# A feed-forward of 11 chunks with three pairs of chunks in Strassen's scheme instead of two

## The reference

```python
def swiglu(h, w_gate, w_up, w_down):          # w_gate, w_up: 1024 x 2816, w_down: 2816 x 1024
    return (jax.nn.silu(h @ w_gate) * (h @ w_up)) @ w_down

for l in range(DEPTH):                        # DEPTH = 2
    x = x + 0.5 * swiglu(rms_norm(x, ffn1_norm[l]), ffn1_w_gate[l], ffn1_w_up[l], ffn1_w_down[l])
    h = rms_norm(x, mix_norm[l])
    z = h @ w_in[l]                           # -> q, k, v of 8 heads, and p
    ...
    x = x + jnp.concatenate([a, m], axis=-1) @ w_out[l]
    x = x + 0.5 * swiglu(rms_norm(x, ffn2_norm[l]), ffn2_w_gate[l], ffn2_w_up[l], ffn2_w_down[l])
return rms_norm(x, final_norm)
```

## Time and profile before

| | |
|---|---|
| median of 3 runs | 915.77 us |
| profiled execution | 916.29 us, of which the span of the trace 914.50 us |
| granted clock of TensorE | 0.999 of full speed |
| busy share of the span | PE 99%, PEld 81%, DVE 77%, ACT 59%, POOL 5% |
| DMA | 180.76 MB, mean 198 GB/s |

### The profile page before, as it was taken

One profiled execution on the slowest core, in us unless ns is written; L12 is line 12 of the kernel. 1 busy time (PEld: TensorE's weight loads), 2 busy tenths in 40 slices (PEclk: granted clock), 3 DMA queues, 4 the chain that ended last, 5 costly groups with the idle time before them and its releaser, 6 DMA issues.

```text
span 914.5 us, 12693 instructions
## 1 busy us (share of the span) xinstructions
PE 905.3 (99%) x4217; PEld 741.0 (81%) x4217; DVE 704.0 (77%) x946; ACT 539.3 (59%) x793; POOL 47.1 (5%) x78
## 2 busy tenths in 40 slices
PE   8999999999999999999999999999999999999997
PEld 6788888887878888888888888888877888888886
DVE  5999599459757998597489986975787588968954
ACT  6775366457638566465385655644675496555633
POOL 1010010010001010100010101010100001001000
PEclk9999999999999999999999999999999999999999
DMA  7966747755245857675267676676434277675831
GB/s 244 347 170 233 275 92 278 240 176 186 93 126 166 307 116 277 213 216 211 92 227 280 141 278 199 207 235 232 138 141 145 84 265 230 218 273 118 274 116 47
DMA packets 131101, 180.76 MB, mean 198 GB/s; under 512 B 7664, under 2 KB 107296, under 8 KB 131056
## 3 DMA queue, kind: packets, MB, share of 16 engines
q1 hardware_dynamic: 117744, 165.43, 52.4%
q0 software_dynamic: 9984, 11.22, 7.4%
q10 hardware_dynamic: 3328, 3.54, 1.2%
HBM read 179.11 MB, written 2.07 MB: 198 GB/s over the span
## 4 chain that ended last, share of the span: by engine, by line
PE 94%; DMA 2%; DVE 2%; ACT 1%; SPq 1%; issue 1%; POOLq 0%; DVEq 0%; POOL 0%; ACTq 0%
PE ps L1397 28%; PE ps L1400 28%; PE ps L1398 28%; PE ps L1506 2%; DMA w_raw<-in_ffn_w_up_dram 1%; PE ps L1458 1%; PE ps L1407 1%; PE ps L1408 1%; PE ps L1480 1%; PE ps L1696 1%; PE ps L1712 1%; PE ps L1724 1%; PE ps L1740 1%; DMA w_raw_f<-in_ffn_w_up_dram 1%; SPq L376 0%
## 5 line engine op out<-in xcount | busy, mean ns | idle before, releaser
L984 DVE TENSOR_TENSOR w_lo<-w_raw,w_hi 128x1024 fp32r<-128x1024 f32 x184 | 216.5, 1218 | 86.4 <-ACT w_hi L627 85.9
L627 ACT ACTIVATE w_hi<-w_raw 128x1024 fp32r<-128x1024 f32 x168 | 167.2, 1049 | 91.0 <-PE ps L1400 91.0
L1397 PE MATMUL ps<-w_hi,gt_hi 128*128 128x512 f32 (+1 forms) x356 | 138.8, 390 | 0.0
L1398 PE MATMUL ps<-w_lo,gt_hi 128*128 128x512 f32 (+1 forms) x356 | 137.7, 387 | 0.0
L1397 PE MATMUL ps<-w_hi,xs_hi 128*128 128x512 f32 x288 | 114.0, 396 | 0.0
L1400 PE MATMUL ps<-w_hi,xs_lo 128*128 128x512 f32 x288 | 112.4, 390 | 0.0
L1398 PE MATMUL ps<-w_lo,xs_hi 128*128 128x512 f32 x288 | 112.2, 390 | 0.0
L1397 PE MATMUL ps<-w_hi,xt_hi 128*128 128x512 f32 x272 | 110.0, 404 | 1.0 <-DVE xt_lo L1009 0.8
L1400 PE MATMUL ps<-w_hi,gt_lo 128*128 128x512 f32 (+1 forms) x356 | 109.8, 387 | 0.0
L1398 PE MATMUL ps<-w_lo,xt_hi 128*128 128x512 f32 x272 | 106.1, 390 | 0.0
L1400 PE MATMUL ps<-w_hi,xt_lo 128*128 128x512 f32 x272 | 101.0, 391 | 0.0
(11 more groups left out here) (151 smaller groups left out, 1487.9 us busy)
## 6 DMA issues: line engine op xcount, KB each, us to landing
w_raw<-in_ffn_w_down_dram SPq DMA_DIRECT2D x72, 512.0 KB, 5.4
w_raw<-in_ffn_w_gate_dram SPq DMA_DIRECT2D x62, 512.0 KB, 4.6
w_raw<-in_ffn_w_up_dram SPq DMA_DIRECT2D x62, 512.0 KB, 5.7
w_raw<-in_w_in_dram SPq DMA_DIRECT2D x32, 512.0 KB, 4.7
w_raw_f<-in_ffn_w_gate_dram SPq DMA_DIRECT2D x16, 512.0 KB, 5.3
w_raw_f<-in_ffn_w_up_dram SPq DMA_DIRECT2D x16, 512.0 KB, 6.2
w_raw_e<-in_ffn_w_down_dram SPq DMA_DIRECT2D x16, 512.0 KB, 7.0
w_raw<-in_w_out_dram SPq DMA_DIRECT2D x16, 512.0 KB, 5.2
```

The source lines that it names most:

```text
L627: nc.scalar.activation(w_hi[slot][:, part], w_raw[raw][:, part], ACT.Copy).then_inc(hi_ready[slot], 2)
L984: nc.vector.tensor_tensor(w_lo[slot][:, part], w_raw[raw][:, part], w_hi[slot][:, part].bitcast(F32), ALU.subtract).then_inc(lo_ready[slot ...
L1397: nc.tensor.matmul(o, hi, wh, start=start, stop=False)
L1398: nc.tensor.matmul(o, hi, wl, start=False, stop=False)
```

## The change

The 11 chunks are dealt in another way: ordinary are 0, 1, 2, 5 and 8, and the pairs are 3+4, 6+7 and 9+10. Each pair now has one ordinary chunk ahead of it, whose transposes and down product lie inside the pair, and the last pair ends the feed-forward. The pair's seven products, seven combines and their order are the same. The loop is gone on all engines: the rounds are written one after the other. Which unit lies in which raw tile and which split place is read from two tables, `RAWS` and `SPLITS`; in the loop the places repeated with each body.

At the end, the down product of chunk 8 does only its first token tile between T2 and T3; its second comes after T4, in two parts with the transposes of `gated_x` between them and those of `gated` behind. The split of `d9` is cut in its two halves on DVE. Smaller: places e and f swap their addresses; the final norm's gain is loaded into a raw tile that has become free, when the last pair's third sum is done; the load of the pooling matrix moves to the start of each mix stage, that of the mask into `load_params`; the loads of the attention bias wait for the last pair's T3.

```diff
-SLOT_E, SLOT_F = 3, 4
-BODIES = 2
-N_ORDINARY = 3 + 2 * BODIES
+SLOT_F, SLOT_E = 3, 4
+PAIRS = 3
+N_ORDINARY = 2 + PAIRS
...
+SPLITS = dict(a=("0a", "1a", "B21.0", "T4.0", "B21.1", "T4.1", "B21.2", "T4.2", "d10"),
...
+              e=("2a", "B11.0", "T2.0", "5a", "B11.1", "T2.1", "8a", "B11.2", "T2.2", "d9"),
...
+RAWS = dict(a=("0a", "1a", "B11.0", "d3", "B22.1", "8a", "B12.2"),
...
+SUM_IN = dict(T1="B11", T2="B11", T3="B12", T4="B21")
+SPLIT_OF = {unit: (role, k) for role in SPLITS for k, unit in enumerate(SPLITS[role])}
+RAW_OF = {unit: (role, k) for role in RAWS for k, unit in enumerate(RAWS[role])}
...
-        final_gain = sb("final_gain", [P, D_MODEL])
+        sb("feed_forward_rest", [P, D_MODEL])
+        final_gain = w_raw[FF2["d"]][:, 0:D_MODEL]
...
+                summed(0, 2)
+                gate_up("5a", 5, 0)
+                split("d2")
+                gate_up("5b", 5, 1)
+                summed(0, 3)
+                down(3)
+                split("T3.0")
+                down(4)
+                split("T4.0")
+                gate_up("B11.1", 7, 0)
...
+                          (gu_ready[1], ord_no(layer, ff, j + 3) + 1))
+                unit(f"d{following}", (down_used, down_no(layer, ff, y + 2)))
+            def last_pair(layer, ff):
+                j, x, y = PAIRS - 1, LAST - 1, LAST
+                n = pair_no(layer, ff, j)
+                pair_begun(layer, ff, j)
+                split_unit(layer, ff, f"d{x}", (m_ready, 7 * n + 5))
+                act.wait_ge(combined, 7 * n + 4)
+                silu_pair(p1, 0, 1)
+                if (layer, ff) == (DEPTH - 1, FF2):
+                    load_final_gain(layer, ff)
+                act.wait_ge(combined, 7 * n + 6)
+                silu_pair(m5, 1, 0)
+                act.wait_ge(combined, 7 * n + 7)
+                silu_pair(u, 1, 1)
+                store_gt_hi(layer, ff, x, 1)
+                split_unit(layer, ff, f"d{y}", (m_ready, 7 * n + 7))
+                store_gt_hi(layer, ff, y)
...
+            def add_units(layer, ff, into, other):
+                tile = w_raw[raw_of(layer, ff, into)[0]]
+                nc.vector.tensor_tensor(tile[:, :], tile[:, :],
+                                        w_raw[raw_of(layer, ff, other)[0]][:, :], ALU.add
+                                        ).then_inc(sum_ready, 1)
...
+            def first_sum(layer, ff, j):
+                slot, n = raw_of(layer, ff, f"B12.{j}")
+                dve.wait_ge(raw_ready[slot], raw_count(slot, n))
+                split_done(layer, ff, f"B11.{j}")
+                add_units(layer, ff, f"B11.{j}", f"B12.{j}")
...
+                o = 3 * j + 2
                 dve.wait_ge(sum_ready, 3 * n + 1)
-                dve.wait_ge(lo_ready[f], 4 * unit_no(layer, ff["stage"], f, 3 * j) + 5)
-                add_units(e, b)
-                lo(d, 3 * j + 2, d)
-                lo(e, 3 * j + 1, e)
-                store_gt_lo(layer, ff, i)
+                split_done(layer, ff, f"T1.{j}")
+                add_units(layer, ff, f"B11.{j}", f"B22.{j}")
+                unit(layer, ff, f"d{o}")
+                unit(layer, ff, f"T2.{j}")
+                store_gt_lo(layer, ff, o)
+                dve.wait_ge(sum_ready, 3 * n + 2)
+                split_done(layer, ff, f"B21.{j}")
+                add_units(layer, ff, f"B21.{j}", f"B11.{j}")
                 dve.wait_ge(m_copied, 2 * n + 1)
                 dve.wait_ge(m_ready, 7 * n + 3)
                 combine(c11, ps[:, BANK_X, :], p1, ALU.add)
...
                 combine(m5, m5, u, ALU.subtract)
                 dve.wait_ge(combined, 7 * n + 3)
                 combine(p1, ps[:, BANK_Z, :], m5, ALU.add)
-                lo(a, 3 * j + 4, a)
+                unit(layer, ff, f"T4.{j}")
                 gate_pair(p1, gated_x, 0, 1, 4 * n + 2)
-                lo(e, 3 * j + 2, b)
+            def second_column(n):
...
+            def ff_body(layer, ff, j):
+                x, y, following = 3 * j + 3, 3 * j + 4, 3 * j + 5
+                n = pair_no(layer, ff, j)
+                pair_begun(layer, ff, j)
+                unit(layer, ff, f"{following}a")
+                second_column(n)
+                unit(layer, ff, f"{following}b")
+                gate_pair(m5, gated_x, 1, 0, 4 * n + 3)
+                last_block(n)
+                unit(layer, ff, f"d{x}")
                 gate_pair(u, gated, 1, 1, 4 * n + 4)
-                store_gt_lo(layer, ff, i + 1, 1)
-                lo(d, 3 * j + 3, e)
-                store_gt_lo(layer, ff, i + 2)
-                gate(layer, ff, 2 * j + 3, 0)
-                lo(a, 3 * j + 5, a)
-                gate(layer, ff, 2 * j + 3, 1)
-                lo(b, 3 * j + 5, b)
+                store_gt_lo(layer, ff, x, 1)
+                unit(layer, ff, f"d{y}")
+                unit(layer, ff, f"B21.{j + 1}")
+                store_gt_lo(layer, ff, y)
+                unit(layer, ff, f"B11.{j + 1}")
+                gate(layer, ff, j + 3, 0)
+                first_sum(layer, ff, j + 1)
+                gate(layer, ff, j + 3, 1)
+                unit(layer, ff, f"B22.{j + 1}")
+                unit(layer, ff, f"T1.{j + 1}")
+            def last_pair(layer, ff):
+                x, y = LAST - 1, LAST
+                n = pair_no(layer, ff, PAIRS - 1)
+                pair_begun(layer, ff, PAIRS - 1)
+                slot, m = split_of(layer, ff, f"d{x}")
+                raw = raw_of(layer, ff, f"d{x}")[0]
+                split_lo(slot, m, raw=raw, halves=(0,))
+                second_column(n)
+                gate_pair(m5, gated_x, 1, 0, 4 * n + 3)
+                last_block(n)
+                split_lo(slot, m, raw=raw, halves=(1,))
+                gate_pair(u, gated, 1, 1, 4 * n + 4)
+                store_gt_lo(layer, ff, x, 1)
+                unit(layer, ff, f"d{y}")
+                store_gt_lo(layer, ff, y)
...
+            def transpose_x(layer, ff, j):
+                pe.wait_ge(pair_gated, 4 * pair_no(layer, ff, j) + 3)
+                transpose_tiles(gated_x)
+            def transpose_y(layer, ff, j):
+                pe.wait_ge(pair_gated, 4 * pair_no(layer, ff, j) + 4)
+                pe.wait_ge(gt_lo_ready, gt_no(layer, ff, 3 * j + 3) + 1)
+                transpose_tiles(gated)
+            def pair(layer, ff, j):
                 n = pair_no(layer, ff, j)
-                units = (3 * j + 2, 3 * j + 2)
-                ordinary(layer, ff, 2 * j + 2, 0, (a, b), units)
-                transpose_gated(layer, ff, 2 * j + 1)
-                ordinary(layer, ff, 2 * j + 2, 1, (a, b), units)
-                whole_down(layer, ff, i - 1, d, 3 * j + 1)
+                o = 3 * j + 2
                 pe.wait_ge(x_lo_ready, 4 * ff_no(layer, ff) + 4)
...
+                seventh(layer, ff, BANK_X, f"B11.{j}", A11)
...
+                seventh(layer, ff, BANK_X, f"B21.{j}", A12)
...
+                seventh(layer, ff, BANK_Y, f"T2.{j}", S2)
+                whole_down(layer, ff, o, ts=(0, 1) if j < PAIRS - 1 else (0,))
                 pe.wait_ge(combined, 7 * n + 2)
-                seventh(layer, ff, BANK_Y, f, 3 * j + 1, S3)
+                seventh(layer, ff, BANK_Y, f"T3.{j}", S3)
                 pe.wait_ge(combined, 7 * n + 1)
-                seventh(layer, ff, BANK_X, a, 3 * j + 4, A22)
-                units = (3 * j + 2, 3 * j + 2)
...
+                seventh(layer, ff, BANK_X, f"T4.{j}", A22)
...
+                ordinary(layer, ff, 2, 0, 2, {4: lambda: transpose_gated(layer, ff, 1)})
+                ordinary(layer, ff, 2, 1, 2)
+                whole_down(layer, ff, 1)
+                pair(layer, ff, 0)
+                for j in range(1, PAIRS):
+                    x, y, o = 3 * j, 3 * j + 1, 3 * j + 2
+                    n = pair_no(layer, ff, j - 1)
+                    pe.wait_ge(combined, 7 * n + 4)
+                    ordinary(layer, ff, j + 2, 0, o)
+                    transpose_x(layer, ff, j - 1)
+                    pe.wait_ge(combined, 7 * n + 6)
+                    ordinary(layer, ff, j + 2, 1, o, {4: lambda: transpose_y(layer, ff, j - 1)})
+                    whole_down(layer, ff, x, buf=1)
+                    whole_down(layer, ff, y)
+                    pair(layer, ff, j)
+                x, y = LAST - 1, LAST
+                whole_down(layer, ff, LAST - 2, ts=(1,),
+                           after={(1, 0): lambda: transpose_x(layer, ff, PAIRS - 1)})
+                transpose_y(layer, ff, PAIRS - 1)
+                x_slot, n = split_of(layer, ff, f"d{x}")
```

456 lines of the change are left out of this document (217 added, 239 removed).

## The result

The changed kernel takes 909.32 us (median of 4 runs, 908.38 to 910.0); the kernel before, run beside it, took 915.88. The ratio is 0.9927, 95% interval 0.9915 to 0.9939: 6.6 us faster, where 909.3 was predicted.

> The changed kernel itself, for a ratio on the same chip as the two kernels beside it: 909.3 within 0.7 us.

What follows compares the result with a forecast made beforehand. The prediction took PE (TensorE) as the bound: 914.50 - 10.9 (matmuls) - 0.3 (refills) + 4.5 (end waits) = 907.8 us span, 909.6 with 1.79 around it, less 0.3: 909.3 us. Range 904.2 to 915.

Steps and rivals of the forecast that it cites:

- What goes: In each feed-forward 12 fewer matmuls at 0.227 us, 10.9 us in all, and one refill less, 0.3 us.
- What covers the added Vector work: In the rounds Vector's 42.4 us plus up to 5 us of waits fit PE's 47.6 us; priced at 0.
- the first transition: From pair 3+4 to chunk 5, the tightest place: Vector comes 0.7 us ahead of PE at 5b; priced at 0.
- Vector's busy time: Over the kernel, Vector's busy time rises from 704 to about 761 us.
- The wait at the end: Before the transposes of gated, PE waits 1.13 us per feed-forward for Vector's chain, 4.5 us in all; bounds 0 and 8.5.
- Loop to straight code: At the loop's jumps, leaving the loop is worth 0 on PE, as the trace shows no gap there.
- Loads: Raw units and the mix stage's first weights land in time, priced at 0; late loads would cost 23 us.
- The sum: Over the whole span, 914.50 - 10.9 - 0.3 + 4.5 = 907.8 us, giving a predicted time of 909.3 us.
- No wait at the ends: At each feed-forward's end Vector is ahead and the 4.5 us wait is absent: 904.8 us; chance 0.17.
- Small waits in the rounds: At the first transition Vector lacks 0.7 to 2 us, so PE waits in 4 places: 912 to 917 us; chance 0.16.
- Vector sets the rounds: In the 12 rounds Vector's work and waits exceed PE's 47.6 us by 1.5 us: 927 us; chance 0.12.
- The change doesn't deliver: Across many places PE waits as much as the removed matmuls save: 914 to 916 us; chance 0.05.

Runs made afterwards that it cites:

- the second experiment: The kernel before with its loop of two bodies written out on SP, ACT, DVE and PE, nothing else: 915.74 us, ratio 0.9997.
- the first experiment's second run: Rerun of the changed kernel with d9's two half splits moved later on Vector, behind the combines and the gt_lo: 906.21 us, ratio 0.9892 (first run 906.1 us).
- the last version: Changed kernel with d9's half splits later on Vector, T2 rounded before Scalar's second copy, gated_x transposed before d8's second tile: 903.62 us, ratio 0.9867.
- that kernel: The changed kernel with d8's down product whole between T2 and T3, and the transposes of gated_x and gated right behind T4: 917.95 us, ratio 1.0020.

## Why the prediction was right, and where it was not

*What goes.* 48 matmuls at 0.227 us: shown by count (528 in a line) and by worth, since the experiment with fewer matmuls gained in the middle pair their pitch, 2.0 to 2.1 us for nine (no wait appears there).

*What covers the added Vector work.* Shown in the changed kernel (no wait of PE in any round) and by its limit: 2.27 us more at one place of each round come out almost whole in the first round of a feed-forward and not at all in the others. The tightest place is 5b at the first transition, as the prediction had it, but with less to spare. In the second feed-forward:

```profile
348.31 2.35 DVE L1080 TENSOR_TENSOR w_lo_f<-w_raw,w_hi_f 128x1024 fp32r<-128x1024 f32 x2
349.79 0.40 PE L1516 MATMUL ps<-w_hi_f,xs_hi 128*128 128x512 f32 x1
```

A half of a split is 1.22 long, so the first half is done at 349.53, 0.26 us ahead of the matmul; 0.7 was forecast. Read in the same way, the leads there are 0.5 at T2 and 1.0 at T4 and at 5a, for 0.9, 1.4 and 1.4: the order of the places is right, and each lead is 0.4 smaller. Half of that lies where the chain starts (B11's split begins 1.44 us behind the release of its place, 1.25 was reckoned); the rest was not traced. The next two feed-forwards have the same leads, and in the first the one at 5b is 0.05. So the price of 0 came out right with very little to spare. T1, where the extra work shows first, has 0.7 to 0.9 and is not in the prediction's list. (Of the four splits that the section on the change counts behind a pair's first `gt_lo`, its rows show three, `d4`, B21 and B11; `d3` stands ahead of it.)

*Vector's busy time.* Its size was wrong: I counted one sum of units more for each feed-forward, but a pair needs three (T1, T2, T4). 2 x 2.28 more in each of 4 is 18.2 above the 57 forecast; 69.6 came. Most of that difference is that the forecast used the length of each instruction, and busy time counts once what two in a row share (a combine is 0.68 long and 0.60 apart; 60 instructions at 0.08 are 4.8, an estimate). The error cost nothing: the round and the chains had been worked out with all three sums.

*The wait at the end.* Forecast 1.13 in front of the transposes of `gated`, measured 0.94 there and 0.36 in front of those of `gated_x`, 1.30 together. The chain was right link by link (19.3 against 19.1 us from T2's split). What I missed is the smaller wait. By the prediction's own terms the gate that ends it is done 18.1 us behind T1's product and PE gets there at 18.1 too, and the place was left out. It is not a cost of its own: what PE waits there, it no longer waits at the second place. So 1.30 stands against 1.13, 0.17 too little in each feed-forward. That Vector sets both is shown by moving two half splits out of the chain: the waits go, and with two more moves all of them, 5.6 us.

*Loop to straight code.* Worth 0, shown by the second experiment.

*Loads.* PE waits for no raw unit, and in the rounds no load shows. But one load reaches PE by a detour, behind the third feed-forward:

```profile
628.92 2.57 ACT L710 ACTIVATE w_hi<-w_raw,gains 128x512 fp32r<-128x512 f32 x4 [3.46 <-DMA w_raw<-in_w_in_dram]
629.68 2.74 DVE L1091 SCALAR_TENSOR_TENSOR w_lo<-w_raw,gains,w_hi 128x512 fp32r<-128x512 f32 x4 [2.72 <-ACT w_hi L710]
632.33 1.28 DVE L1100 TENSOR_TENSOR resid<-ps,resid 128x512 f32<-128x512 f32 x2
633.07 1.26 PE L1599 MATMUL ps<-ident,resid 128*128 128x128 f32 x8
```

The mix stage's first weights are issued from 617.55 on, 19.4 us before the stage's end, as forecast. But its loads land up to 11.4 us after their issue, where 5.7 was reckoned. Scalar waits for one, Vector's splits follow Scalar, the sum of the residual follows them without a gap, and the transposes of the residual come 0.4 to 0.5 us late. When the kernel ran again they lost nothing, and in the first experiment's second run PE waited 1.2 us there. The prediction priced this at 0. No experiment moved a load, so that this one sets the wait is read from the chain and not shown.

*The smaller changes* (addresses of e and f, the final gain, the mix stage's loads) were not tried alone. The mix stages take 86.13 and 86.35 us, 86.17 and 86.20 before.

*The sum.* 10.9 + 0.3 - 5.2 = 6.0 against 6.2 between the two spans. Small terms that the sum leaves out nearly cancel: the kernel before waited ahead of 5b in each feed-forward, 0.8 us in all by starts, where the earlier trace rows have 0.2, and the changed one doesn't; the residual's transposes took 0.4 to 0.5 of that back, and the mix stages 0.1. That the median agrees with the forecast to a tenth is luck. The forecast's 4.5 was 0.7 too small for the waits, and the span came out 0.5 above the forecast's 907.8. The profiled execution then lay 0.7 above the median of its four, where 0.3 had been taken off. (A group of transposes, 0.435 in the prediction, is 0.44 by its own rows; nothing hangs on it.)

*The rivals.* No wait at the ends: false for this order, and true for the last version (903.6, where 904.8 was worked out for it). Small waits in the rounds: false, none, but by 0.05 to 0.3 us only. Vector sets the rounds: false as forecast, but near. The change doesn't deliver: false, 6.6 us came. With Vector at 90% and weight loads at 147.72 of 179.89, 82%, the section "Identifying the Most-Contended Engine" of the Trainium skill's "Perfetto Trace Analysis" names Vector. Neither engine alone is the bound: 27 us of Vector work more cost 9, 24.5 us of matmuls less gave 9, and 5.6 us came from the order alone. Busy shares say here that both are close; which place decides they don't say.

## What to carry to other kernels

A bilinear scheme that trades matmuls for sums pays only where the vector engine runs ahead, so follow its chain place by place: the start, where it has no lead yet, and the end, where nothing follows that could cover it. At the end put on the chain only what the next wait needs, and keep independent matmuls back as cover. Then check the result by starts, since a short wait shows in the distance of two rows before it shows in a busy share.

## What the runs showed of the hardware

A wait of 0.94 us by starts left the granted clock at 1.00 each time, and so did those of 1.54 us in the experiment with more Vector work and of 1.62 and 1.68 us in the one with fewer matmuls. One of 2.82, behind a continuous run of matmuls and four small transposes, was followed by a clock of 0.54 to 0.62 for 3 to 4 us in three of four cases, and by 1.00 in the fourth, though the four waits are the same to 0.01 us. The nine executions of that kernel spread from 915.93 us at a mean granted clock of 0.997 to 919.32 us at 0.994. So the price of a wait at that place is not the wait alone, and it is not the same each time.
